# A mixture-of-experts stage on Trainium2: loop written out, gate moved from the scatter matrix to the rows, scatter in two f32r products, four more weight chunks held ahead

## The reference, cut to what matters

```
def expert_choice_ffn(h, w_router, w_gate, w_up, w_down):
    cap = CAPACITY_FACTOR * s // N_EXPERTS                         # 64
    aff = jax.nn.softmax((h @ w_router).astype(jnp.float32), axis=-1)
    gate, idx = lax.top_k(aff.transpose(0, 2, 1), cap)
    xe = take_along_axis(h, idx_flat)                              # 16 experts x 64 rows x 1024
    hid = silu(einsum('becd,edf->becf', xe, w_gate)) * einsum('becd,edf->becf', xe, w_up)
    ye = einsum('becf,efd->becd', hid, w_down) * gate[..., None]
    out = jnp.zeros_like(h).at[idx_flat].add(ye)
...
        x = x + gt2 * expert_choice_ffn(h, ...)
```

## Time and profile before

| | us |
|---|---|
| median of 3 runs | 3038.01 |
| profiled execution | 3041.64 |
| its span, first to last instruction | 3039.9 |
| PE busy | 2797.6 (92%) |
| DVE busy | 1053.7 (35%) |
| ACT busy | 777.3 (26%) |
| POOL busy | 626.4 (21%) |
| mean granted TensorE clock | 0.968 of full speed |

### The profile page before, as it was taken

How to read it: one execution, slowest core, us unless ns; L and a number is a source line. 1 busy time by engine, 2 the same in 40 slices (tenths; PEclk the granted TensorE clock), 3 DMA queues, 4 the chain that set the end, 5 groups by cost and what they waited for, 6 DMA issues and landing times.

```text
span 3039.9 us, 35121 instructions
## 1 busy us (share of the span) xinstructions
PE 2797.6 (92%) x14112; PEld 1964.0 (65%) x14112; DVE 1053.7 (35%) x1748; ACT 777.3 (26%) x1389; POOL 626.4 (21%) x290
## 2 busy tenths in 40 slices
PE   4999999979989999799999979999999999899998
PEld 3677777767544447343333349688887797878877
DVE  2455555531430003311111149730004488410034
ACT  2233333321330002100000032632222315522222
POOL 2222222220000000000000014234434331334443
PEclk8999999989999999899999989999999999999999
DMA  8111122110131222489999932122322221223321
GB/s 243 28 55 55 56 72 58 34 59 1 35 128 60 71 81 70 183 340 385 400 400 400 398 131 85 55 70 84 97 97 92 75 84 56 70 83 97 97 83 56
DMA packets 219709, 382.04 MB, mean 126 GB/s; under 512 B 10833, under 2 KB 154069, under 8 KB 219605
## 3 DMA queue, kind: packets, MB, share of 16 engines
q1 hardware_dynamic: 213072, 376.46, 35.2%
q10 hardware_dynamic: 6533, 4.10, 0.5%
HBM read 378.44 MB, written 2.10 MB: 125 GB/s over the span
## 4 chain that ended last, share of the span: by engine, by line
PE 75%; issue 7%; PEld 5%; DVE 4%; ACT 4%; POOL 2%; DMA 1%; DVEq 1%; SPq 1%; PEldq 1%; ACTq 0%; POOLq 0%
PE bank L1665 11%; PE bank L1670 11%; PE bank L1669 11%; PE bank L1601 10%; PE bank L1490 7%; PE bank L1573 2%; PE bank L1591 2%; PE bank L1514 2%; PEld bank L1212 2%; PE bank L1204 2%; PE bank L1270 1%; PE bank L1279 1%; PE bank L1423 1%; PE bank L1344 1%; PE bank L1283 1%
## 5 line engine op out<-in xcount | busy, mean ns | idle before, releaser
L639 POOL TENSOR_TENSOR w_lo<-ring,w_hi 128x2048 fp32r<-128x2048 f32 x96 | 444.3, 4628 | 781.8 <-ACT w_hi L651 781.8
L1665 PE MATMUL bank<-hT_hi,w_hi 128*128 128x512 f32 x864 | 348.1, 403 | 10.2 <-DVE hT_lo L2392 8.7
L651 ACT ACTIVATE w_hi<-ring 128x2048 fp32r<-128x2048 f32 x96 | 184.0, 1916 | 661.7 <-PE bank L1665 640.8
L1669 PE MATMUL bank<-hT_lo,w_hi 128*128 128x512 f32 x864 | 340.3, 394 | 0.0
L1670 PE MATMUL bank<-hT_hi,w_lo 128*128 128x512 f32 x864 | 338.4, 392 | 0.0
L1601 PE MATMUL bank<-ring,xeT 128*64 128x512 f32 x1024 | 233.8, 598 | 9.7 <-issue 6.4
L1665 PEld LDWEIGHTS bank<-hT_hi,w_hi 128*128 128x128 f32 x864 | 163.0, 189 | 48.6 <-DVE hT_lo L2392 9.7
L2583 DVE TENSOR_TENSOR ffn_hT<-ffn_sg,bank 128x512 f32<-128x512 f32 x44 | 30.3, 688 | 461.4 <-PE bank L1670 461.4
L1670 PEld LDWEIGHTS bank<-hT_hi,w_lo 128*128 128x128 f32 x864 | 163.1, 189 | 40.7
L1669 PEld LDWEIGHTS bank<-hT_lo,w_hi 128*128 128x128 f32 x864 | 162.6, 188 | 35.5 <-issue 1.0
L1204 PE MATMUL bank<-hT,head_w 128*128 128x512 f32 x384 | 180.3, 600 | 1.1 <-ACT col_q L726 1.1
(11 more groups left out here) (465 smaller groups left out, 4846.3 us busy)
## 6 DMA issues: line engine op xcount, KB each, us to landing
ring<-in_w_gate SPq DMA_DIRECT2D x86, 1024.0 KB, 6.8
ring<-in_w_up SPq DMA_DIRECT2D x86, 1024.0 KB, 11.5
ring<-in_w_down SPq DMA_DIRECT2D x86, 1024.0 KB, 13.1
ring<-in_w_in SPq DMA_DIRECT2D x33, 1024.0 KB, 5.5
head_w<-in_w_in SPq DMA_DIRECT2D x32, 512.0 KB, 5.3
mod_w<-in_w_mod SPq DMA_DIRECT2D x8, 2048.0 KB, 8.6
ring<-in_w_out SPq DMA_DIRECT2D x12, 1024.0 KB, 5.1
ring<-in_w_mod SPq DMA_DIRECT2D x8, 1024.0 KB, 15.3
```

Source lines behind the costliest of these rows:

```text
L639: pool.tensor_tensor(w_lo[m % 2][:], raw[m % RAW][:], w_hi[m % 2][:].bitcast(F32), ALU.subtract).then_inc(lo_ready, 1)
L651: return act.activation(dst, src, ACT.Copy)
L1665: first = mm(dst, a[0], b[0], start=start, stop=False)
L1669: mm(dst, a[0], b[1], start=False, stop=False)
```

## The change

1. The expert pairs are written out on all engines, in place of the loops; the drains behind gate, up and down are gone, ACT and DVE wait for counts of `chunk_used` instead (`expert_done`). The ninth block of `onehot` and the ninth gather are gone.
2. The scatter matrix is a 0/1 matrix in f32r, made anew for each pair (`slots_of`: one f32r product of 512 columns and four fp32 products of 16 columns), and the gate multiplies the rows: `ye` = down result x `gate_col` x `gt2_b`. `affT`, `scat`, `gate_b`, the eight double products of pair 0 and GpSimd's copies are gone.
3. `ye` is split in two f32r parts (ACT copies `ye_hi`, DVE subtracts `ye_lo`), and each scatter piece is two f32r products. Their places between the chunk pairs move: none after the first of gate, then 1, 2, 2, and 2, 1 behind those of up.
4. The gather is in two halves: one before the transposes of `hid`, one after them. ACT copies `hidT` before it scales its half of the gathered rows.
5. Four chunks of pair 0 (up, the first two chunk pairs) are loaded into memory of their own as soon as the last router product is done, besides the eight in the ring; the ring's count is four less.

The diff, cut to its core:

```diff
+EXTRA = 4
+N_LAYER = N_EXPERT + PAIRS * PER_PAIR - EXTRA
...
+        def ring_base(pair):
+            return N_EXPERT + (pair * PER_PAIR - EXTRA if pair else 0)
+
+        def expert_done(eng, pair, part):
+            chunks = (8, 16, 24)[part] - (EXTRA if part and pair == 0 else 0)
+            eng.wait_ge(chunk_used, ring_base(pair) + chunks)
...
+                            if pair == 0 and part == 1 and i < EXTRA:
+                                if i == 0:
+                                    reached(sp, f"router_done_{TT - 1}")
+                                dst = extra[i][:, :].rearrange("p (k n) -> p k n", k=2)
+                                sp.dma_start(dst, src).then_inc(sem("extra_in"), 16)
+                            else:
+                                load(n, wide(n), src)
+                                n += 1
...
-            with pool.Fori(0, PAIRS) as pair:
-                pool.wait_ge(sem("ye_ready"), pair + 1)
-                pool.tensor_copy(scat_now[:].unsqueeze(1), scat[:, bass.ds(pair, 1), :]).then_inc(sem("scat_taken"), 1)
...
# ACT
+            reached(act, "route_consts")
+            copy(pair_sel_r[:], pair_sel[:])
+            reached(act, "slot_turned")
+            copy(slotT_r[:], slotT[:]).then_inc(step["sel_ready"], 1)
+            def split_ye(pair):
+                for hf in range(2):
+                    c = slice(hf * 512, hf * 512 + 512)
+                    act.wait_ge(sem("ye_gated"), pair * 2 + hf + 1)
+                    copy(ye_hi[:, c], ye[:, c]).then_inc(sem("ye_hi_ready"), 1)
+            gathered(0)
+            for pair in range(PAIRS):
+                if pair:
+                    split_ye(pair - 1)
+                expert_done(act, pair, 0)
...
+                copy(hidT[:, 0:4, :].rearrange("p k n -> p (k n)"), bank[0][:]).then_inc(sem("hidT_act"), 1)
+                if pair + 1 < PAIRS:
+                    gathered(pair + 1)
+            split_ye(PAIRS - 1)
...
# TensorE
+            def slots_of(pair):
+                if pair:
+                    pe.wait_ge(sem("x_added"), pair * 8)
+                else:
+                    pe.wait_ge(sem("xeT_dve"), 1)
+                    pe.wait_ge(sem("xeT_act"), 1)
+                    reached(pe, "sel_ready")
+                mm(bank[5][:], pair_sel_r[:, pair, :], slotT_r[:], start=True, stop=True)
+                for t in range(TT):
+                    last = mm(bank[4][:, 0:EXPERTS], onehot[:, t, pair * P:(pair + 1) * P], aff[:, t, :], start=t == 0, stop=t == TT - 1)
+                last.then_inc(sem("slots_done"), 1)
...
+                rows, cols = scat_now[:, t * P:(t + 1) * P], slice(hf * 512, (hf + 1) * 512)
+                mm(dst, rows, ye_hi[:, cols], start=True, stop=False)
+                mm(dst, rows, ye_lo[:, cols], start=False, stop=True).then_inc(sem("scattered"), 1)
...
                 for j in range(4):
+                    chunk_pair(0, xeT, 0, j)
+                    if pair:
+                        scatter_behind(pair - 1, ((), (0,), (1, 2), (3, 4))[j])
                 for j in range(4):
+                    chunk_pair(1, xeT, 2, j)
+                    if pair:
+                        scatter_behind(pair - 1, ((5, 6), (7,), (), ())[j])
+                    if j == 2:
+                        slots_of(pair)
+                if pair + 1 < PAIRS:
+                    pe.wait_ge(sem("onehot_ready"), 2)
+                    pe.wait_ge(sem("scat_ready"), pair + 1)
+                    gather(pair + 1, 0)
                 for k in range(KD):
+                    pe.wait_ge(sem("hid_ready"), pair * 2 + k // 4 + 1)
                     last = pe.transpose(...)
+                if pair + 1 < PAIRS:
+                    gather(pair + 1, 1)
                 pe.wait_ge(sem("hidT_act"), pair + 1)
                 pe.wait_ge(sem("hidT_dve"), pair + 1)
                 for j in range(4):
+                    chunk_pair(2, hidT, 6, j)
...
# DVE
+                dve.wait_ge(sem("slots_done"), pair + 1)
+                for a in range(2):
+                    e = 2 * pair + a
+                    copy(gate_col[a * 64:a * 64 + 64, :], bank[4][a * 64:a * 64 + 64, e:e + 1])
+                ts(scat_now[:], bank[5][:], iota_p[:], None, ALU.is_equal).then_inc(sem("scat_ready"), 1)
+                expert_done(dve, pair, 1)
...
+                    stt(ye[:, c], bank[6 + hf][:], gate_col[:], gt2_b[:, c], ALU.mult, ALU.mult).then_inc(sem("ye_gated"), 1)
+                for hf in range(2):
+                    c = slice(hf * 512, hf * 512 + 512)
+                    dve.wait_ge(sem("ye_hi_ready"), pair * 2 + hf + 1)
+                    tt(ye_lo[:, c], ye[:, c], ye_hi[:, c].bitcast(F32), ALU.subtract).then_inc(sem("ye_ready"), 1)
```

More of the change, by code:

```diff
@@ L1567, in _, with gather @@
             reached(pe, "route_consts")
-            def gather(pair):
-                for k in range(KD):
+            def gather(pair, half):
+                for k in range(4 * half, 4 * half + 4):
                     for t in range(TT):
-                        sel = onehot[:, t, pair * P:(pair + 1) * P] if isinstance(pair, int) else onehot[:, t, bass.ds(pair * P, P)]
-                        last = mm(bank[4 + k // 4][:, k % 4 * P:(k % 4 + 1) * P], xn[:, t, k * P:(k + 1) * P], sel,
-                                  start=t == 0, stop=t == TT - 1)
+                        last = mm(bank[4 + half][:, k % 4 * P:(k % 4 + 1) * P], xn[:, t, k * P:(k + 1) * P],
+                                  onehot[:, t, pair * P:(pair + 1) * P], start=t == 0, stop=t == TT - 1)
@@ new lines, in scatter_behind, with chunk_pair @@
+            def scatter_behind(pair, pieces):
+                for piece in pieces:
+                    if piece >= 2:
+                        pe.wait_ge(sem("x_added"), pair * 8 + piece - 1)
+                    scatter(pair, piece, bank[4 + piece % 2][:])
+            pe.wait_ge(sem("onehot_ready"), 1)
+            for half in range(2):
+                gather(0, half)
+            for pair in range(PAIRS):
+                def chunk_pair(part, lhs, banks, j):
+                    chunk = []
+                    for a in range(2):
+                        i = 8 * part + 2 * j + a
+                        if pair == 0 and 8 <= i < 8 + EXTRA:
+                            pe.wait_ge(sem("extra_in"), 16 * EXTRA)
+                            chunk.append(extra[i - 8][:, :].rearrange("p (k n) -> p k n", k=2))
+                        else:
+                            n = ring_base(pair) + i - (EXTRA if pair == 0 and i >= 8 else 0)
+                            arrived(pe, n)
+                            chunk.append(wide(n))
@@ L1601, in chunk_pair @@
                                 last = mm(bank[banks + hf][a * 64:a * 64 + 64, :], lhs[:, 2 * j + kk, a * 64:a * 64 + 64],
-                                          wide(n + a)[:, kk, hf * 512:(hf + 1) * 512], start=2 * j + kk == 0, stop=2 * j + kk == 7)
-                                if kk == 1 and hf == 1:
+                                          chunk[a][:, kk, hf * 512:(hf + 1) * 512], start=2 * j + kk == 0, stop=2 * j + kk == 7)
+                                if kk == 1 and hf == 1 and not (pair == 0 and part == 1 and 2 * j < EXTRA):
                                     last.then_inc(chunk_used, 1)
[L1606 to L1617, removed]
                 pe.wait_ge(sem("xeT_act"), pair + 1)
@@ L2344, in add_scattered @@
                 tt(x[:, t, c], x[:, t, c], src, ALU.add).then_inc(sem("x_added"), 1)
[L2346 to L2347 removed]
+            gathered(0)
+            one_hot(2, EXPERTS)
+            for pair in range(PAIRS):
+                if pair:
                     for piece in range(8):
                         add_scattered(pair - 1, piece, bank[4 + piece % 2][:])
[L2350 to L2355 removed]
+                dve.wait_ge(sem("slots_done"), pair + 1)
[4 more added lines that the diff above has]
+                expert_done(dve, pair, 1)
                 for hf in range(2):
```

151 lines of the change are left out of this document (43 added, 108 removed).

## The result

The changed kernel takes 3000.16 us in the median of 4 executions (2996.68 to 3003.63), the kernel before 3038.6 in the same series: ratio 0.9874, 95% interval 0.9856 to 0.9891. Forecast were 3000.6 and a range of 2992 to 3015. The gain is 38.4 us; forecast were 37.4.

The account below looks back on a forecast made before the run. PE was taken to set the pace before the change, DMA to set the end after it. From 3038.0 us, 32.9 off up to the end of down and 4.5 off the tail gave 3000.6, range 2992 to 3015.

Parts of the forecast that it names:

- tail: From the end of down to block 2's first product: first sum of squares 4.5 us earlier, bounds 0 and 6.
- PE's own turn: PE's need in each of pairs 1 to 6: a sum of 56.7 us, under DMA's 61.4.
- DMA's idle time in pair 0: Before the first down chunks come free in pair 0, DMA was to idle about 7 us.
- The sign of being wrong that hung on block 2: The forecast is wrong if block 2, 1235.6 us, is not as long as before.
- PE's turn at the upper bounds: PE's need per pair with scatters at their upper bound and slots at 1.6: 61.2 us, under DMA's 61.4.
- the cover of the critical stretch: Between up and down, where no chunk comes free: 14.8 us of loads in flight against 14.4 needed, 0.4 to spare.
- PE sets the pace: In the kernel before, PE's work and gaps make the pair's 63.3 us, and DMA stands idle 2 us a pair.
- The one idle us: DMA idle charged between up and down: 0.15 us for each of 7 pairs, bounds 0 and 14.
- The four chunks: Four chunks of pair 0 loaded ahead: worth some 3 us, not the 10 of their bytes.
- Rival B: DMA still runs dry in each gather: 1 to 2 us by 7 pairs, 3007 to 3014 us; chance 0.22.
- Rival C: The clock falls to 1.2 GHz in PE's new waits: 3067 us with a quarter of each pair; chance 0.03.
- Rival D: PE remains the bound, as f32r products cost what fp32 ones do: no gain to speak of; chance 0.03.

Follow-up runs that it names:

- experiment 1, half loads: The changed kernel, with each chunk's load from pair 2 on bringing only the first half of its columns: 2965.37 us, ratio 0.9765.

## Why the prediction was right, point by point, and where it was not

The sum came out nearly term by term, from the first gate product on: first down chunk reissued 42.2 after it, measured 41.1 (1288.37); from there to the end of down 439.0, measured 438.7; first sum of squares 6.1 later, measured 5.9; tail 4.5 shorter, measured 5.0. PE's own turn was put at 56.7 and is 56.59, by terms that were off both ways: the eight scatter pieces take 4.7 and not 4.0, `slots_of` 1.4 and not 1.1, gather and transposes 8.2 and not 8.7, and chunk pairs that follow each other without anything between 3.45 and not 3.58. DMA's idle time in pair 0 was about 5.8 us (147 of 412 GB/s over 9 us) and not 7.

That the total came within 1 us is in part luck. The stage gave 34.5 us where 32.9 to the end of down were forecast, and the tail 0.5 more than forecast; block 2, put at 0, took 1.9 more. The sign of being wrong that hung on block 2 can't be read either way, as its length wanders by 6.5 us with the same code. Two sums of mine were wrong without effect. PE's turn at the upper bounds, with slots at 1.6, is 61.7 and not 61.2, so over DMA's 61.4 and not under it. And the cover of the critical stretch was weighed against 2.1 us for issue and start, where I had put 2.5 to starting a line before; with 2.5 nothing is left of the 0.4.

"PE sets the pace" is the step that did not hold. I read the chain of the earlier trace rows and the sum 58.9 + 3.4 = 63.3 as PE's total being the bound, with DMA idle for 2 us as the consequence. As a description of the looped kernel that stands: from pair 2 on none of PE's waits is put down to a load. What was wrong is what I took from it, that the pair gets shorter by whatever PE is relieved of. Taking 0.53 a turn off PE's gap gave nothing, and moving work without shortening it gave 13.1 us. As soon as PE waits for landings, the hole bounds the turn:

| kernel | hole, us | turn, us |
|---|---|---|
| changed kernel | 10.94 | 61.4, one of 62.8 |
| gather whole | 12.2 | 61.5 to 62.0, two longer; mean of six 62.2 |
| gather whole, fp32 scatter | 12.2 | 61.8 to 62.4, mean 62.1 |
| before, written out, scatter moved | 12.7 | 61.9 to 62.2 |
| before, written out | 14.5 | 63.9 |
| changed, 3.7 us added in the hole | 14.5 | 63.8 to 64.0, one of 65.5 |

From 12.7 us on each us of the hole is one us of the turn, by the line 61.4 + (hole - 12.0), which I drew through the last three rows. The two kernels at 12.2 lie half a us above it, so where exactly DMA begins to run dry is known only to within that. The forecast survived its wrong reading because its second half asked the right question, whether the cover of that stretch holds. It had 0.4 us to spare by my working. By the runs it is 1.1 if one goes by the line (12.0 - 10.94), and 0.6 if one goes by the kernels at 12.2 (1.3 more hole, 0.7 more turn); both are estimates. The one idle us that I had charged for this came in another way: one of the five full turns is 1.4 longer (SP's first gate issues at 1532.77 and 1595.59). DMA moves its 408 to 410 GB/s meanwhile, and PE waits 1.25 us for the first gate chunk pair, which it does in no other of these turns. The other kernels with a hole of 10.9 and whole loads have such a turn too, of 62.3 to 62.9 us. What causes it is open. The looped kernel before has a hole of 14.8 and a turn of 63.3, where the table would give 64.2; what makes it 0.9 better than its line is open too. So it is shown that the hole was the bound once the loop was written out, and not shown that it was the bound of the looped kernel.

Where the gain came from, then, in the stage: 34.5 us, of which 18.2 up to the first down chunk's reissue (the 16 row products took 15.3 of it; PE's waits of 1.57 and 1.23 us before and behind the gather are gone too, and `slots_of` takes 1.4 back) and 16.3 behind: 4.7 from the first turn, 60.2 instead of 64.8, 8.1 from the next five, 61.4 to 62.8 instead of 63.3, with a last scatter piece and a wait of 0.87 moved out of the hole, and 3.5 from the end, which comes one chunk pair after the last landing. The four chunks: forecast some 3, measured 5.0. The f32r product: nothing. The tail: POOL's copies.

Rival B, DMA dry in each gather, did not come about as the kernel stands, but the runs with the gather whole and with added work show it at 12.2 and 14.5 of hole. Rival C, the clock: PE's 45 waits of up to 1.5 us left the granted clock at 1.00. In two of the experiments it fell in the stage, once in each, behind waits for loads of 1.92 and 1.46 us, for one chunk pair that then took 5.3 us and not 3.65. The Trainium skill, TensorE: Matmul & The Clock Gate, "HAM oscillation — how this bites in real kernels", has waits for DMA throttle the products behind them at every tile, with waits of 3 to 5 us. Those two falls agree with it in kind. But they came once in each kernel, behind other waits there of 1.8 and 2.6 us the chunk pair took its 3.65, and in the changed kernel the clock did not fall, so C did not decide the time. Rival D is excluded by the half loads: PE needs 56.6. On the loops, the Trainium skill, Runtime: NRT & Kernel Launch, "Instruction fetch mechanics", says that a taken branch can stop the fetch and that kernels prefer to be written out where possible. The gap at the head of the turn did shrink from 0.94 to 0.41; the time did not.

## What to carry to other kernels

With a ring of buffers, ask for each period how long no buffer comes free, and hold that against what is in flight at its start; a bound of this kind hides behind an engine that is busy nearly all the time, and the cure is to shorten that stretch, by moving work out of it. Work elsewhere in the turn was nearly free here, up to the 4.8 us of waits that PE had: 3.7 us in each of six turns cost 1.6 us in all in one place and 15.2 in the other. Bytes loaded ahead are worth their full time only if DMA then has no idle time left to absorb them.

## What the runs showed of the hardware

A change between fp32 and f32r on PE is not free. At full clock f32r products of 512 columns start 0.23 us apart; the first one behind fp32 products starts 0.34 before the next f32r one, or 0.43 before the next fp32 one, and the last of a group 0.33 before the fp32 product behind it (experiment 1, half loads). DMA held 409 GB/s over whole turns and did not slow for never resting. The granted clock stayed at 1.00 over 45 waits for DMA of up to 1.5 us in the changed kernel, and fell to 0.50 for about 3.5 us behind a wait of 1.92 us in one experiment and of 1.46 in another. In the same two kernels it stayed at 1.00 behind waits of 2.62 and 1.81, so the length of the wait alone does not decide it. Written out, the program took 90 packets and 1.47 MB on the instruction queue instead of 76 and 1.25 MB, and beside full DMA none of PE's waits in the stage is put down to fetching: they end on loads (31.4 us), `xeT` (1.6), `hidT` (0.8) and `hid` (0.8).
